# Writing 128 copies of twelve distance bias rows head by head during the up products, in place of one transfer among the delta rule steps

## The reference

```
bias = jnp.take(bias_a, t5_bucket(kpos[None, :] - qpos[:, None]), axis=0)     # 4 heads, 256 x 256 each
s1 = jnp.einsum('bhqd,bhkd->bhqk', q1, k1).astype(jnp.float32) + bias
...
bias = jnp.take(bias_b, t5_bucket(off * dil), axis=0).transpose(2, 0, 1)      # 8 heads, three dilations
```

## Time and profile before

| | us |
|---|---|
| median of 3 runs | 2328.2 (2315.79 to 2331.55) |
| the profiled execution, its own time | 2328.16 |
| its span, first to last instruction | 2326.4 |
| TensorE busy | 1814.8 (78%) |
| VectorE busy | 469.3 (20%) |
| ScalarE busy | 307.6 (13%) |
| GpSimd busy | 28.8 (1%) |
| mean granted TensorE clock | 0.842 |

### The profile page before, as it was taken

One profiled execution on the slowest core, in us unless ns is written; L12 is line 12 of the kernel. 1 busy time (PEld: TensorE's weight loads), 2 busy tenths in 40 slices (PEclk: granted clock), 3 DMA queues, 4 the chain that ended last, 5 costly groups with the idle time before them and its releaser, 6 DMA issues.

```text
span 2326.4 us, 29082 instructions
## 1 busy us (share of the span) xinstructions
PE 1814.8 (78%) x12246; PEld 975.5 (42%) x12246; DVE 469.3 (20%) x1096; ACT 307.6 (13%) x726; POOL 28.8 (1%) x38
## 2 busy tenths in 40 slices
PE   7899999999999999987666666655675666566565
PEld 6675886577488747642212212211221221122122
DVE  2334331253432213530101010100101010010011
ACT  2232221032311102420000000000000000000001
POOL 0010000001010000000000000000000000000000
PEclk9899999999999999987777777777767767676777
DMA  7543443432364346359999999999999999999998
GB/s 244 97 139 127 145 152 128 153 127 98 109 190 145 130 161 247 132 213 403 406 426 423 421 425 425 425 424 426 424 415 425 425 419 424 425 424 424 425 425 334
DMA packets 146422, 693.78 MB, mean 298 GB/s; under 512 B 12732, under 2 KB 62460, under 8 KB 92978
## 3 DMA queue, kind: packets, MB, share of 16 engines
q1 hardware_dynamic: 143346, 683.68, 73.2%
q0 software_dynamic: 2864, 9.00, 2.0%
q10 hardware_dynamic: 144, 0.13, 0.0%
HBM read 688.57 MB, written 4.19 MB: 298 GB/s over the span
## 4 chain that ended last, share of the span: by engine, by line
PE 49%; DMA 40%; SPq 4%; DVE 3%; issue 2%; DVEq 1%; ACT 1%; ACTq 0%
DMA arena<-in_w_up 30%; PE bank L565 16%; DMA arena<-in_w_down 9%; PE bank L588 6%; PE bank L691 6%; PE bank L1097 5%; PE bank L1114 3%; SPq L399 2%; SPq L407 1%; PE bank L890 1%; PE bank L686 1%; PE bank L976 1%; PE bank L914 1%; PE bank L972 1%; DVE arena L1853 1%
## 5 line engine op out<-in xcount | busy, mean ns | idle before, releaser
L1097 PE MATMUL bank<-arena 128*32 128x512 f32 (+1 forms) x3072 | 502.9, 811 | 311.1 <-DMA arena<-in_w_up 293.6
L1097 PEld LDWEIGHTS bank<-arena 128*32 128x32 f32 x3072 | 113.6, 144 | 696.7 <-DMA arena<-in_w_up 418.6
L565 PE MATMUL bank<-arena 128*128 128x256 f32 (+1 forms) x2208 | 383.1, 335 | 7.4 <-ACT arena L1142 3.4
L565 PEld LDWEIGHTS bank<-arena 128*128 128x128 f32 x2208 | 346.1, 192 | 46.4 <-ACT arena L1142 4.6
L1114 PE MATMUL bank<-arena 128*32 128x256 f32 x2816 | 237.5, 484 | 95.0 <-DMA arena<-in_w_down 94.9
L1853 DVE TENSOR_TENSOR arena<-arena,bank 64x256 f32<-64x256 f32 x96 | 40.1, 418 | 772.0 <-ACT arena L1376 770.3
L1114 PEld LDWEIGHTS bank<-arena 128*32 128x32 f32 x2816 | 94.9, 132 | 215.4 <-DMA arena<-in_w_down 132.7
L588 PE MATMUL bank<-arena 128*128 128x512 f32 x352 | 152.0, 591 | 0.0
L691 PE MATMUL bank<-arena 128*128 128x256 f32 x576 | 145.6, 401 | 0.0
L1376 ACT ACTIVATE arena<-bank 64x512 f32<-64x512 f32 (+1 forms) x48 | 23.2, 549 | 823.7 <-PE bank L1097 823.7
L691 PEld LDWEIGHTS bank<-arena 128*128 128x128 f32 x576 | 109.7, 198 | 20.8 <-issue 4.6
(11 more groups left out here) (277 smaller groups left out, 1166.2 us busy)
## 6 DMA issues: line engine op xcount, KB each, us to landing
arena<-in_w_gate SPq DMA_DIRECT2D x128, 1408.0 KB, 19.3
arena<-in_w_up SPq DMA_DIRECT2D x128, 1408.0 KB, 22.3
arena<-in_w_down SPq DMA_DIRECT2D x144, 1024.0 KB, 9.3
arena<-in_w_down SPq DMA_DIRECT2D x32, 1536.0 KB, 12.0
arena<-in_w_up SPq DMA_DIRECT2D x44, 1024.0 KB, 7.0
arena<-in_w_in SPq DMA_DIRECT2D x40, 1024.0 KB, 7.4
arena<-in_w_out SPq DMA_DIRECT2D x12, 1024.0 KB, 7.0
arena<-in_w_down SPq DMA_DIRECT2D x12, 512.0 KB, 3.3
```

Of the source, the lines that this page charges most:

```text
L565: last = mm(ps[bank][:, j * S + lo:j * S + lo + n], w[:, k, c:c + P], xT[:, k, lo:lo + n], start=(k == 0), stop=(k == KT - 1))
L1097: last = mm(ps[b][32 * q:32 * q + 32, 0:n], expert_x[:, k, :], weights[:, q // 2, c:c + n], start=(k == 0), stop=(k == KT - 1))
```

## The change

The transfer leaves its place ahead of POOL's loop over the layers. In layer 1, behind the three operations on the queries, stand twelve transfers instead, one per head, of 128 copies x 2 KB = 256 KB. Transfer h waits until 4 + h up products are done. The wait for all of them becomes 16 x 12.

```diff
@@ -461,9 +461,6 @@
             pool.dma_start(const[:, 2 * P + 4:NC], a["consts"][:, 2 * P + 4:NC]).then_inc(sem("const_in"), 16)


-            pool.wait_ge(sem("bias_copied"), 1)
-            pool.wait_ge(sem("key_products"), 2)
-            pool.dma_start(scratch.rearrange("h (p n) -> h p n", p=P), distance_bias[0:BIAS_HEADS, :].unsqueeze(1).broadcast_to([BIAS_HEADS, P, 2 * S])).then_inc(sem("bias_out"), 16)
             for l in range(DEPTH):

                 pool.wait_ge(sem("q_shuffled"), at(l, "q_shuffled", 1))
@@ -472,11 +469,16 @@
                 nc.gpsimd.tensor_tensor(att_q, att_q, table("cos").unsqueeze(1).broadcast_to([P, 4, S]), ALU.mult)
                 pool.drain()
                 nc.gpsimd.tensor_tensor(att_q, att_q, q_swapped, ALU.add).then_inc(sem("q_rotated"), 1)
+                if l == 0:
+                    pool.wait_ge(sem("bias_copied"), 1)
+                    for h in range(BIAS_HEADS):
+                        pool.wait_ge(sem("up_product"), 4 + h)
+                        pool.dma_start(scratch[h:h + 1, :].rearrange("o (p n) -> o p n", p=P), distance_bias[h:h + 1, :].unsqueeze(1).broadcast_to([1, P, 2 * S])).then_inc(sem("bias_out"), 16)


             pool.wait_ge(sem("rows_used"), DEPTH * ROW_UNITS + 1)
             pool.dma_start(gain, a["norm1_g_2"].broadcast_to([P, D])).then_inc(sem("gain_in1"), 16)
-            pool.wait_ge(sem("bias_out"), 16)
+            pool.wait_ge(sem("bias_out"), 16 * BIAS_HEADS)
```

## The result

| | before | changed |
|---|---|---|
| median of the runs, us | 2326.91 (4 runs, 2315.79 to 2331.55) | 2353.26 (4 runs, 2346.59 to 2354.91) |
| ratio, 95% interval | | 1.0114 (1.0081 to 1.0147) |
| profiled execution, own time / span, us | 2328.16 / 2326.4 | 2346.59 / 2344.6 |

The changed kernel is 26 us slower (1.1%). The forecast was 2384, 56 us slower. The sign was right and the time lies in the range, but the loss is less than half of what the sum gave.

What follows compares the result with a forecast made beforehand. TensorE was taken to bound the first half of the span, where the copy lies, full DMA engines the second. The sum -11 + 38 + 25 + 4 = +56 on 2328.16 us gave 2384, range 2313 to 2412 (forecast's own 2350 to 2410).

Steps and rivals of the forecast that it cites:

- The gain, -11: Layer 1's delta rule stage loses its 11.2 us, including a 9.02 us TensorE gap inferred as a delayed instruction packet.
- The length of a copy, 10.3 us: Each 256 KB copy reads one partition over one path at 24.7 to 26.5 GB/s; bounds 2.4 and 45.8 us.
- That copies hold all sixteen engines, and weights starve: In layer 1's up products, copies keep the engines; 64 KB of a 2048 KB weight unit pass per 256 KB copy.
- The stops, 38 + 25 us: TensorE stands in layer 1's up products 38 us for weight unit 5, then 25 us for unit 7.
- One path for all heads: Copies 0 to 6 in layer 1's up products were summed one after another, 7 x 10.3 = 72 us.
- The order at the start: Weight unit 5, issued at 249.5 us, comes behind the first copy, released at 249.0, with 41 us of cover.
- The sum's third step: Late in layer 1's up products: last copy to 401 us, unit 9 in by 405, wanted at 417; cost 0.
- The lower clock, +4: After each of two TensorE stops in layer 1's up products, a lower clock costs 2.1 us.
- Read back, POOL, down products at 0: The read back's wait, POOL's rotations and extra issues, and the down products behind the copies each cost 0.
- Rival 1: Copies among layer 1's up products are short (2.4 us) and hidden, leaving only the 11.2 us gain: 2317 us; chance 0.30.
- rival 2: One partition limits each copy among the up products to 45.8 us: 2776 us; chance 0.03.
- Rival 3: Copies of 5 to 6 us or small weight bursts, unit 5 late once by 10 to 30 us: 2320 to 2348; chance 0.07.

Runs made afterwards that it cites:

- e1: Kernel before, with its one 3072 KB transfer kept whole but moved to the 4th up product of layer 1; 2315.8 us, ratio 0.9958.
- e5: Kernel before, with the transfer cut into twelve by head, all issued at the old place, the second key_products of layer 1; 2379.74 us, ratio 1.0227.
- e11: Kernel before, old place, three transfers of four heads, rows in partitions 0 to 3, 32 to 35 and 64 to 67; 2348.6 us, ratio 1.0101.
- e9: Changed kernel, with all twelve transfers reading the row of head 0, so one partition; 2363.72 us, ratio 1.0161.
- e2: Kernel before, old place, rows spread to partitions 0, 4, ..., 28 and 64, 68, 72, 76, in two transfers; 2314.16 us, ratio 0.9954.
- e12: Changed kernel, with all twelve transfers at the 4th up product at once, heads in the order 0, 4, 8, 1, 5, 9, ...; 2321.48 us, ratio 0.9986.
- e7: Changed kernel, with all twelve transfers waiting for the 4th up product only, heads in their usual order; 2374.64 us, ratio 1.0196.
- e6: Changed kernel, with only the order of heads altered to 0, 4, 8, 1, 5, 9, ...; 2316.13 us, ratio 0.9957.
- e10: Changed kernel, with each transfer one up product earlier, h waiting for 3 + h; 2351.5 us, ratio 1.0111.
- e8: Changed kernel, but cut by rows: eight transfers of 16 copies of all twelve heads, at the 4th to 11th up product; 2315.21 us, ratio 0.9952.

## Why the prediction was right in sign and wrong in size

- **The gain, -11:** right. e1 has 11.2 us. That an instruction packet was what waited had been inferred and is still not shown alone, but the queues bear it out: in the gap of before, in the three of e5 and in that of e11 (the last 2.7 us of 8.6) the one q8 packet comes as the gap ends, and the gaps of e5 (15.3 to 19.3 us, the copies' queue at 90.0% of the engines' time in the first) are longer than that of before (9.02 us at 66.9%).
- **The length of a copy, 10.3 us:** right. One path gives 26.2 GB/s over 95 us (e9), 10.0 us a copy, and 30 GB/s, 8.7 us, while a copy has all engines. e2 excludes that the engines or HBM set it. The step behind it, four heads to a path and three paths, has its rows at e12, and an engine to a head at e11. The choice between 2.4 and 45.8 us, the costliest one in the sum, held.
- **That copies hold all sixteen engines, and weights starve:** right (share 100% at 242 to 246 us, landings up to 71 us).
- **The stops, 38 + 25 us: this step failed.** They measured 33.4 us, in one stop. The sum took one packet for one, which the earlier trace rows show while both queues are full, for as long as any copy waits, so 64 KB of weights to 256 KB of copy. That holds inside a copy (30 and 31 packets) and not between two (777 packets of weights and 33 of copies). In the 64.7 us before the stop 4.24 MB of weights passed beside 1.86 MB of copies; one for one is 0.47, a ninth. So units 5 and 6 came through and only unit 7 was late. A copy of 256 KB has 64 packets of 4 KB, on average four to an engine; an engine that is through with them seems to serve weights until the next copy's packets reach it. In e7, where all copies are there from the start, these stretches shrink and the stop is 54.2 us. Why a copy's packets come several us after its issue is not shown. On one path (e9) the stop is 44.7 us instead of 63: this is 18 us of the error, some 3 of them from 10.0 instead of 10.3 us a copy.
- **One path for all heads:** the second half of the same error. The sum lined the twelve copies up one behind the other, though it had itself derived three paths. With heads on several paths the stop is 11.3 us shorter (44.7 to 33.4), and in another order it is gone (e6). Two paths at work where some engines are still at head 3 and others at head 4 would explain it: e7's copies go at 44 GB/s in place of 26 where head 4 follows head 3 (e12). The rows show the rates, not the engines. Three paths and an order were enough to ask what neighbours share.
- **The order at the start:** wrong, without weight. The sum put unit 5 behind the first copy; SP issued it at 235.5, 0.5 us ahead of it. e10 puts it behind, and the stops stay 35 us. (The sum's third step has unit 9 wanted at 417, where its own steps give 382 + 4 x 6.96 = 410. Unit 9 is in by 405 there, so nothing hangs on it.)
- **The lower clock, +4:** one stop instead of two, 1.8 us. Behind the gap of before, 0.50 was granted.
- **Read back, POOL, down products at 0:** right; L487 is issued at 661.84 and waits for nothing of the copies, layer 2's up products are 142.66 us again.

With measured sizes the sum is -11.2 + 33.4 + 1.8 = +24, against 26.4 between the medians. (Between the two profiled executions it is 18.4; 2.9 us of the early start and 2.7 us in the experts, behind the last read back, make up the rest.) Rival 1 was wrong on the rate, rival 2 too. Rival 3, bursts of weights and one late unit, is the nearest to the mechanism of the part that failed, and its 2348 the nearest end; it had been given 0.07. The bursts are not small, though (0.78 MB in 4 us), and the unit is unit 7, issued four products later than unit 5. That the time came just inside the forecast's own 2350 to 2410 is luck: the lower edge stood there for copies of 7 us, and the copies took 8.7 to 10.

## What to carry to other kernels

In this kernel a transfer's cost to its neighbours was the time for which it held the engines, not its bytes (the same 3072 KB made TensorE wait 54.2 us for weights in e7, 3.6 in e12, not at all in e1): leave a broadcast whole (e1), or cut it so that every piece still reads from many partitions (e8), spread its rows (e2), or at least let neighbouring pieces read from different groups (e6); each gave 0.4 to 0.5%. When two streams share the engines, do not carry the ratio of a window in which both are full over a stretch in which they are not; count what each queue moved. A wait called issue beside a slow transfer is worth a look at the instruction queue's packets in that window, and on GpSimd at the landing of its own transfers.

## What the runs showed of the hardware that was not expected

- While a slow transfer holds the engines, TensorE can stand until an instruction packet has come: 9 us before, 15.3, 19.3 and 16.9 us in e5 (the link to the packet is inferred from its time).
- GpSimd, at a `drain` with a transfer of its own under way, went on 0.8 us (e5) and 0.3 us (e11) after that transfer had landed, 27.0 and 41.8 us late.
- SyncE's issue of a transfer of w_up, 0.4 to 0.6 us in the kernel before, stood for 27.4 us in the changed kernel and 47.4 us in e7 while copies held the engines.
- At the start of a copy the ratio is not one for one: from 94.8 to 101.2 us of the kernel before, the copy moved 112 packets and the weights 24, later 216 and 216. Why the beginning differs was not tried.
